# A hybrid attention and mLSTM step on one core: first tiles in eight pieces, gate rows through DRAM, and three pieces of work in another order

## The reference, cut to what matters

```python
xn = _rms(x, g_pre)                       # x: 1024 prompt tokens and 8 x 8 sample tokens, 1024 features
proj = xn @ w_in
qa, ka, va, za, qm, km, vm, om, zm, ig, fg = jnp.split(proj, SPLIT_POINTS, axis=-1)
att, wk, wv = attend(qa, ka, va, sinks)   # window of 128 keys, ALiBi bias, sinks, softmax
a_out = att * jax.nn.silu(za)
i_pre = ig + bg[:M_HEADS]                 # 4 input gates and 4 forget gates a token
logf = jax.nn.log_sigmoid(fg + bg[M_HEADS:])
h, C, n, m = _mlstm(qm, km * (M_HEAD_DIM ** -0.5), vm, i_pre, logf, C0, n0, m0)   # chunks of 128 tokens
m_out = jax.nn.sigmoid(om) * _rms(h, g_mh) * jax.nn.silu(zm)
y = jnp.concatenate([a_out, m_out], axis=-1) @ w_out
return x + _rms(y, g_post), (wk, wv, C, n, m)
```

## Time and profile before

| what | value |
|---|---|
| time, median of 3 runs | 556.85 us (555.76 to 557.73) |
| the profiled execution's own time | 556.09 us |
| its span, first to last instruction | 554.3 us |
| mean granted clock of TensorE | 0.999 of full speed (the level of 2.4 GHz) |
| PE busy | 544.9 us (98%) |
| DVE, ACT, POOL busy | 303.7, 236.2, 145.1 us |
| HBM traffic | 43.35 MB read, 8.07 MB written |

### The profile page before, as it was taken

How to read it: one execution, slowest core, us unless ns; L and a number is a source line. 1 busy time by engine, 2 the same in 40 slices (tenths; PEclk the granted TensorE clock), 3 DMA queues, 4 the chain that set the end, 5 groups by cost and what they waited for, 6 DMA issues and landing times.

```text
span 554.3 us, 9995 instructions
## 1 busy us (share of the span) xinstructions
PE 544.9 (98%) x3957; PEld 507.8 (92%) x3957; DVE 303.7 (55%) x591; ACT 236.2 (43%) x631; POOL 145.1 (26%) x143
## 2 busy tenths in 40 slices
PE   8999999999999999999999999999999999999995
PEld 7999999999999999999989898999999998888783
DVE  4830001493656556521276767434676766878497
ACT  6952221423454434431266666343413225545451
POOL 3011121112234233332011312145533532001041
PEclk9999999999999999999999999999999999999999
DMA  8762211733121011015114222471121003202336
GB/s 337 281 206 76 68 40 44 218 129 90 40 41 39 4 39 39 3 39 151 42 40 132 77 81 57 117 310 69 40 74 41 1 0 115 76 2 84 126 106 253
DMA packets 38319, 51.60 MB, mean 93 GB/s; under 512 B 13338, under 2 KB 28962, under 8 KB 37618
## 3 DMA queue, kind: packets, MB, share of 16 engines
q1 hardware_dynamic: 29410, 50.94, 27.6%
q10 hardware_dynamic: 8864, 0.04, 0.9%
HBM read 43.35 MB, written 8.07 MB: 93 GB/s over the span
## 4 chain that ended last, share of the span: by engine, by line
PE 90%; DVE 3%; DMA 2%; issue 2%; ACT 1%; POOL 0%; SPq 0%; DVEq 0%; POOLq 0%; ACTq 0%
PE ps L687 49%; PE ps L615 3%; PE ps L616 3%; PE ps L617 3%; PE ps L942 3%; PE ps L944 3%; PE ps L943 3%; PE ps L658 2%; PE ps L734 2%; PE ps L794 2%; PE ps L835 1%; PE ps L878 1%; PE ps L868 1%; PE ps L663 1%; DMA first<-in_first 1%
## 5 line engine op out<-in xcount | busy, mean ns | idle before, releaser
L687 PE MATMUL ps<-x_hl,w_hi 128*128 128x364 f32 (+1 forms) x1104 | 277.0, 332 | 0.0
L687 PEld LDWEIGHTS ps<-x_hl,w_hi 128*128 128x128 f32 x1104 | 193.1, 188 | 4.9 <-issue 4.5
L687 PE MATMUL ps<-x_hl,w_lo 128*128 128x364 f32 (+1 forms) x552 | 181.2, 328 | 0.0
L687 PEld LDWEIGHTS ps<-x_hl,w_lo 128*128 128x128 f32 x552 | 103.8, 188 | 0.0
L1931 POOL TENSOR_TENSOR qmT<-qmT,sg 128x364 f32<-128x364 f32 (+1 forms) x24 | 35.2, 1465 | 48.8 <-DVE sg L1726 29.0
L1094 ACT ACTIVATE prob<-prob,nmx 128x192 f32<-128x192 f32 (+1 forms) x64 | 28.0, 438 | 44.5 <-DVE sd L1495 44.5
L1883 POOL TENSOR_TENSOR prob<-prob,rden 128x768 f32<-128x768 f32 (+1 forms) x16 | 22.6, 1414 | 70.9 <-DVE rden L1501 70.9
L1043 ACT ACTIVATE sg<-zx 128x364 f32<-128x364 f32 (+1 forms) x24 | 12.2, 507 | 67.2 <-DVE zx L1383 67.2
L381 POOL TENSOR_TENSOR w_lo<-w_raw,w_hi 128x1024 fp32r<-128x1024 f32 x12 | 28.7, 2395 | 45.8 <-ACT w_hi L1028 38.1
L615 PE MATMUL ps<-wt_hi,x_hl 128*128 128x324 f32 x128 | 39.9, 312 | 0.0
L617 PE MATMUL ps<-wt_hi,x_hl 128*128 128x324 f32 x128 | 39.8, 311 | 0.0
(11 more groups left out here) (298 smaller groups left out, 999.7 us busy)
## 6 DMA issues: line engine op xcount, KB each, us to landing
w_raw<-in_w_in_tiles SPq DMA_DIRECT2D x23, 512.0 KB, 3.6
x_tok<-in_x_prompt SPq DMA_DIRECT2D x8, 512.0 KB, 5.4
x_res<-in_x_prompt SPq DMA_DIRECT2D x7, 512.0 KB, 4.3
wt_raw<-in_w_tok SPq DMA_DIRECT2D x4, 648.0 KB, 9.0
logw<-lw_rows SPq DMA_DIRECT2D x8, 256.0 KB, 3.9
Cs<-in_state_C SPq DMA_DIRECT2D x16, 128.0 KB, 2.3
out_C_sample<-Cs SPq DMA_DIRECT2D x16, 128.0 KB, 1.9
wq_a<-in_w_out_blocks SPq DMA_DIRECT2D x2, 1024.0 KB, 6.6
```

The costliest lines, as they stand in the source:

```text
L687: last = mm(ps[:, sub_bank(sub), 0:w], wt, xm, start=(at_ == 0), stop=(at_ == 23))
```

## The change

- `PARTS` has eight pieces of one feature group each, where it had two of one and three of two. The first piece's `w_hi` is made by DVE, the others' still by ACT.
- The norms' row goes to DRAM straight from `stat`, element by element; the two transposes and DVE's two copies go, and DVE makes `rstd_q` after the last token tile.
- The gates go to DRAM element by element after each token tile (18 small stores in all), and come back as rows `gi` by two loads. The nine transposes of `gates` go. The gates' tensor is packed (8 values a token, no padding to 32), and the bias additions read SBUF where they read PSUM.
- `scores(it + 1)` is issued between `prob_transposes(it - 1)` and `values(it - 2)`; `values` does its products over 64 keys first and those over 128 after.
- In the mLSTM round of the sample tokens DVE's `splits` comes after `h_scale`.
- `norm` is cut into `norm_scale` and `norm_residual`; in the last pair DVE adds bank and `y_odd` (`c22_done`) between the two.

```diff
-PARTS = [(0, 1), (1, 2), (2, 4), (4, 6), (6, 8)]
+PARTS = [(kk, kk + 1) for kk in range(KT)]
...
+        def store_gates(t):
+            off, n = x_cols(t)
+            wait(sp, "tok_dve", t + 1)
+            for q in range(2):
+                sp.dma_start(gate_rows[q, :, off:off + n].rearrange("h p -> p h"), gates[0:n, t, q * MH:(q + 1) * MH],
+                             allow_slow_non_contiguous=True).then_inc(s("gi_st"), 16)
+
+        for t in range(NC - 1):
+            store_gates(t)
+        wait(sp, "rstd_ready", NTILE)
+        sp.dma_start(rs_row[0, 0:T_P].rearrange("(c p) -> p c", p=P), stat[:, NTILE:NTILE + NC], allow_slow_non_contiguous=True)\
...
         sp.wait_ge(s("rs_st"), 32)
         sp.dma_start(rstd_b[:], rs_row[0, :].partition_broadcast(P)).then_inc(s("rstd_ld"), 16)
-        wait(sp, "tok_done", NTILE)
+        for t in range(NC - 1, NTILE):
+            store_gates(t)
         sp.dma_start(resets[:], i["resets"]).then_inc(s("resets_ld"), 16)
-        wait(sp, "rows_ps", 1)
+        sp.wait_ge(s("gi_st"), 32 * NTILE)
+        for q in range(2):
+            sp.dma_start(gi[:, q, :], gate_rows[q]).then_inc(s("gi_ld"), 16)
         load_w(4)
...
-            if t == NC - 2:
-                rstd_transposes()
...
-        project(24)
-        wait(pe, "rstd_b", 1)
-        wait(pe, "tok_dve", NTILE)
-        wait(pe, "tok_act", NTILE)
-        for c in range(NTILE):
-            _, n = x_cols(c)
-            last = nc.tensor.transpose(ps[0:PQ + MH, c // 4, (c % 4) * P:(c % 4) * P + n], gates[0:n, c, 0:PQ + MH], ident[0:n, 0:n])
-        last.then_inc(s("rows_ps"), 1)
-        project(24 * 7)
-        project(24 * (S_P2 - N_EARLY - 8))
+        project(24 * (S_P2 - N_EARLY))
...
+        scores(0)
         for it in range(S_P3 - S_P2):
-            if it < N_ATT:
-                scores(it)
             project(24)
             if 1 <= it <= N_ATT:
                 prob_transposes(it - 1)
+            if it + 1 < N_ATT:
+                scores(it + 1)
             if 2 <= it <= N_ATT + 1:
                 values(it - 2)
...
         for q, (k0, k1) in enumerate(PARTS):
-            first_hi(q)
+            if q >= 1:
+                wait(act, "first_hi", q)
+                first_hi(q)
             x_hi(0, range(k0, k1))
...
+        dve.wait_ge(s("first_ld0"), 16)
+        CP(w_hi[:, :, w_cols(0)], w_raw_part(0)).then_inc(s("first_hi"), 1)
...
-        wait(dve, "rows_ps", 1)
-        for dst, bias, q in ((ib, bgi, 0), (fb, bgf, PQ)):
-            last = TS(dst[:], ps[q:q + MH, 0:3, :].rearrange("p b t -> p (b t)")[:, 0:T], bias[q:q + MH, 0:1], None, ALU.add)
+        dve.wait_ge(s("gi_ld"), 32)
+        TS(ib, ib, bgi[:, 0:1], None, ALU.add)
+        last = TS(fb, fb, bgf[:, 0:1], None, ALU.add)
...
-            if it >= 1:
+            if it >= 1 and done != 0:
                 splits(S_P3 + it - 1)
...
             if done is not None:
                 h_scale(done)
+            if done == 0:
+                splits(S_P3 + it - 1)
...
             else:
-                norm(first_of(p - 1) + 1)
+                norm_scale(first_of(p - 1) + 1)
             wait(dve, "prod", product("P5", p) + 1)
             wait(dve, "v7_done", p + 1)
             TT(q[1][:, 512:D], ps[:, 2 * p, :], q[1][:, 512:D], ALU.add).then_inc(s("c22_done"), 1)
+            if end_:
+                norm_residual(first_of(p - 1) + 1)
```

More of the change, by code:

```diff
@@ L208, in build @@
     tok_lo = sb("tok_lo", [T_S, 2, TOK_H], F32, Dr + 8 * KT * TOK_W + 4096)
-    gates = sb("gates", [P, NTILE, 2 * PQ], F32, GI + 9984)
-    row = [sb(f"row{n}", [MH, T], F32, Dr + n * 4 * T) for n in range(6)]
-    ib, fb, ra, rb, rc, rd = row
+    gates = sb("gates", [P, NTILE, 2 * MH], F32, GI + 9984)
+    row = [sb(f"row{n}", [MH, T], F32, Dr + n * 4 * T) for n in range(4)]
+    ra, rb, rc, rd = row
+    gi = sb("gi", [MH, 2, T], F32, Fr + 4 * T)
+    ib, fb = gi[:, 0, :], gi[:, 1, :]
     NR = 3 * PQ + MH
@@ L789, in values @@
                 else:
[L790 to L794, removed]
                     for h in range(2):
@@ L799, in values @@
                                 rows, half = slice(kv * HD, (kv + 1) * HD), slice(g * HQ, (g + 1) * HQ)
-                                last = mm(head(g, rows, h), v[half, rows], probT[half, u % 2, 1, kv * P + h * HQ:kv * P + (h + 1) * HQ],
-                                          start=False, stop=True, skip_group_check=True)
+                                mm(head(g, rows, h), v[half, rows], probT[half, u % 2, 1, kv * P + h * HQ:kv * P + (h + 1) * HQ],
+                                   start=(h == 0), stop=False, skip_group_check=True)
+                    for g, h in ((0, 0), (0, 1), (1, 0), (1, 1)):
+                        v = va[:, blk - 1 + g] if g == h else va_sh[:, blk]
+                        for kv in range(KVH):
+                            rows, c0 = slice(kv * HD, (kv + 1) * HD), (2 * kv + g) * P + h * HQ
+                            last = mm(head(g, rows, h), v[:, rows], probT[:, u % 2, 0, c0:c0 + HQ], start=False, stop=True, skip_group_check=True)
             else:
@@ L1401, in token_evac @@
                         in1=tok_lo[:, q, 0:2 * MD].rearrange("p (h v) -> p h v", h=2), op0=ALU.mult, op1=ALU.add)
-                    last = add(gates[0:n, t, q * PQ:q * PQ + MH], 1, TOK_H - 2 * MH + q * MH, MH)
+                last = add(gates[0:n, t, :], 1, TOK_H - 2 * MH, 2 * MH)
                 last.then_inc(s("tok_dve"), 1)
@@ L1406, in token_evac @@
             TS(va[0:n, t, VA0:KV_W], second[:, 2 * MD:2 * MD + KV_W - VA0], r, None, ALU.mult)
-            if t == 0:
-                wait(dve, "zeros", 1)
-            TS(gates[0:n, t, :].rearrange("p (q h) -> p q h", q=2)[:, :, 0:MH],
-               second[:, TOK_H - 2 * MH:TOK_H].rearrange("p (q h) -> p q h", q=2), r, None, ALU.mult).then_inc(s("tok_dve"), 1)
-        def rstd_evac():
-            wait(dve, "rstd_ps", 1)
-            CP(rstd_r[:, 0:P], ps[0:NC, 0, 0:P])
-            CP(rstd_r[0:1, P:P + T_S], ps[0:1, 0, P:P + T_S]).then_inc(s("rstd_b"), 1)
-            TS(rstd_q[:], stat[:, NTILE:NTILE + NC], float(HD) ** -0.5, None, ALU.mult).then_inc(s("rstd_b"), 1)
+            TS(gates[0:n, t, :], second[:, TOK_H - 2 * MH:TOK_H], r, None, ALU.mult).then_inc(s("tok_dve"), 1)
         V.memset(warm[:], 0.0).then_inc(s("warm_zero"), 1)
+        dve.wait_ge(s("first_ld0"), 16)
+        CP(w_hi[:, :, w_cols(0)], w_raw_part(0)).then_inc(s("first_hi"), 1)
         for q, (k0, k1) in enumerate(PARTS):
@@ L1473, in score @@
                 dve.wait_ge(s("att_ld"), 80)
-                wait(dve, "rstd_b", 2)
+                wait(dve, "rstd_b", 1)
             if u < 2 * NC:
@@ L1845, in _ @@
         Q.memset(ones[:], 1.0)
-        Q.memset(gates[:], 0.0).then_inc(s("zeros"), 1)
         for q in range(len(PARTS)):
@@ L1851, in _ @@
         wait(pool, "w1_lo", len(PARTS))
-        Q.memset(vm1[:, :, :, MD:W1], 1.0).then_inc(s("zeros"), 1)
+        Q.memset(vm1[:, :, :, MD:W1], 1.0)
         for t in range(NTILE):
```

40 lines of the change are left out of this document (20 added, 20 removed).

## The result

The changed kernel takes 581.75 us (median of 4 runs, 578.18 to 584.37), the kernel before 557.05 us in runs on the same chip (4 runs, 555.76 to 557.73). The ratio is 1.0442, with a 95% interval of 1.0377 to 1.0507: slower, by 24.7 us, where I had forecast 5 us less, and far outside my range. The profiled execution took 580.28 us, its span is 578.5 us, and TensorE's mean granted clock is 0.973, where it was 0.999.

The account below looks back on a forecast made before the run. PE, busy 98% of the span, was taken as the bound. Gains of 2.0 + 1.57 + 0.3 + 0.6 + 0.6 = 5.1 us gave 551.0 from 556.09 or 551.8 from 556.85; forecast 551.4 us, 8-in-10 range 549.5 to 554.0.

Parts of the forecast that it names:

- The start: First pair's first span: eight smaller pieces let PE finish it near 14.4 instead of 16.36, gaining 2.0 us.
- The transposes: Norms' two and gates' nine transposes come off PE whole: 0.45 and 1.12 us, together 1.57 us.
- What takes their place: Gate rows through DRAM: store landing 3.2 us, load 2.5, row chain 3 us late but covered.
- The slack: Ahead of first scores at 131.82: gate rows have 4.9 us left; norms' row, some 4 us later, is wanted at 131.8.
- The rival: Gate rows too late: 8 us per trip, chain 13 us late, 8 us stall against 5 gained, 559.5 us; chance 0.06.
- My sign of a wrong prediction: At the first scores: PE waiting there for the gate rows would show the prediction wrong.
- Attention: Reordered scores and values: two iterations with block 0's values save one shape change each, 0.3 us; usual iterations gain nothing.
- Sample tokens: DVE's weight split moved behind the head scaling lets PE transpose hs earlier, gaining 0.6 us.
- Last pair: DVE's residual moved behind the addition PE waits for, gaining 0.6 us at the end.

Follow-up runs that it names:

- start_only: Kernel before with only the eight-piece start and the first piece's w_hi on DVE: 553.44 us, ratio 0.9962.
- both_rows_no_pe: rows_by_pe with gates transposed by DVE in 32 x 32 blocks, moved SBUF to SBUF by eight DMAs, and norms by two scattered stores: 550.28 us, ratio 0.9894.
- gates_block_t: rows_by_pe with gates transposed by DVE in 32 x 32 blocks and moved SBUF to SBUF by eight DMAs; norms through PE: 550.90 us, ratio 0.9906.
- rows_by_pe: Changed kernel with only the DRAM rows undone, so gates and norms become rows through PE's transposes: 551.83 us, ratio 0.9941.
- probes: Three kernels adding seven DMAs each to rows_by_pe, each waited for before the next, to time small stores and loads; own times 561 to 578 us.

## Why the prediction was wrong, point by point

- **The start** (2.0 forecast): 2.38 by the trace, and 2.4 us for `start_only`. The size is near, the way to it only in part: I let piece 3 (counted from 0) land at 8.2 us, and ACT had it at 7.4. PE's only wait, 0.5 us, is at piece 2; from there it ran almost without gaps. My reading of the Trainium skill's advice to batch (DMA: Bandwidth & Descriptors, section Bandwidth), a fixed part paid one after the other, would have made this term a loss of 4 us; this case's trace does not agree with that reading, with eight loads issued back to back. The Trainium skill states the 2.0 us in another section of that page, Anatomy of one DMA, for the GpSimd path, and these loads were issued by SP.
- **The transposes** (1.57): 0.44 and 1.12 came off PE whole.
- **What takes their place** is the step that failed. The prediction said: "The trace has no scattered 4-byte store to DRAM. The nearest are the element-wise loads of `r2c`, which landed in 2.1 to 3.9 us; I take their median, 3.2." A store of as many touching words takes 8.7 us or more by itself; behind others, the last landed 15.4 us after issue, and the norms' 64 words 17.6. A load was put in the place of a store, and one in the place of eighteen. The bound of 3.9 was no bound: nothing in the trace excluded a larger value. The load back took 3.4 us, above the 2.5 that I had taken and inside its bounds. The gates of the last tile but one were ready at 88.5 us, and SP came to them at 109.5, when the norms' stores had landed, a wait that my chain had left out; the same small stores in another order, or on another engine's queue, were not tried.
- **The slack.** I had the norms' row "some 4 us later" than 85.91 and "wanted at 131.8". Its load was issued at 109.1, 23 us later, and the row is wanted by 99.0: POOL's split of tile 3 (2.34) is behind the scaling (2.47), and PE stood from 103.8 on. I had looked for the readers of the row and not for what stands behind the reader on its engine. For the gates I had 4.9 us at the first scores; ACT's evacuation decides earlier, at 108.1 us, which leaves DVE's step a start of 105.2, and `both_rows_no_pe` and `gates_block_t`, which started it at 103.5 and 104.3, had no such stop. That is 5.5 us from the 99.7 of `rows_by_pe`, so the size was near and the place wrong. My sign of a wrong prediction, a wait at the first scores, did not show: the stops began 54 and 33 us ahead of them.
- **The rival** had the mechanism, late gate rows, with a trip of 8 us for each way and 559.5 us. Its rule held at the real size: DVE's step on the rows started at 132.0, 32.3 us late against `rows_by_pe`; less the 5.5 of slack that is 26.8, which are the 24.4 us of stops and the 2.5 that 17 matmuls between them lost at the lower clock. What ran slow behind the second stop, 2.9 us, was in no sum. Its chance, 0.06, followed from the borrowed price. The Trainium skill's sentence beside it, that transfers under 512 B become read-modify-write (DMA: Bandwidth & Descriptors, section Specifications), was the warning, but size is not what decides here: 4-byte words 64 bytes apart took 2.6 us. Nearer is a sentence of the Trainium skill that the prediction left out: VectorE: DVE Perf Modes, section The three transpose paths, calls a plain strided DMA copy used as a transpose a trap, 19 times slower than the DMA's crossbar path when the innermost stride of the destination is large. No run here used the crossbar, so none shows that factor. Against the same words in 32-byte runs the transposing store took 9.9 us for 2.8, and words 512 bytes apart took 2.7: a large distance between words was no harm here.
- **Attention** (0.3): 0.52. I had nothing for the usual iterations, and there nine of them take 6.47 us each where they took 6.50, 0.2 us in all. **Sample tokens** (0.6): 0.55. **Last pair** (0.6): 0.7. The waits for `hs` and `y_odd` went and none came in their place.

The terms of the forecast sum to 5.1 us, and to 5.7 by the trace. With the gates' rows by a trip that is in time, 550.3 to 550.9 us was measured, 5.4 to 6.1 us below the kernel before on the same chip, where I had forecast 551.4 for the change.

## What to carry to other kernels

When a change has an operation that the trace does not show, measure that operation or treat its price as unbounded above; a bound from another direction (a load for a store) or another shape is none. In these probes a transposing store to DRAM cost by how many separate writes fell into one small stretch, not by bytes or elements, and an element-wise load by its words: let DVE turn blocks of 32 x 32 first and move runs of 128 bytes. And when a transfer is late, ask what stands behind its reader in that engine's program, since that comes due first; the longest wait on PE's list names where it stopped, not why.

## What the runs showed of the hardware that was not expected

- 256 touching 4-byte words from 128 partitions to DRAM take 8.7 us, 2048 take 11.0, and 1024 words 64 bytes apart 2.6.
- An issue behind many such stores stalls the issuing engine: one of 64 words took 8.46 us on SP, and one of the gate stores 6.4. With nothing in flight, in the probes, none took over 0.7.
- 4352 words loaded twice into 4 partitions take 32.5 us, 3.7 ns a word; 1024 words into 128 partitions take 3.9 us, 2.5 ns a word beyond the 1.3 us of a load of four runs.
- After an idle of 14.7 and one of 9.7 us PE ran about 17 and 20 matmuls at the lower clock level, which cost 5.3 us in all.
- One DVE instruction transposes 128 x 288 floats in blocks of 32 x 32 in 0.48 us.
